# A decoder layer on one core: a second HBM accumulator for the routed experts, and their whole down product in rounded FP32

## The chip, the cores and the metric

The kernel runs on one core of a Trainium2 chip. The metric is the device time of one execution in microseconds (us), the median of 3 runs. One more execution was taken by the hardware profiler; the rows shown below come from it.

The engines are named as the profile names them: PE (TensorE, matrix products; PEld is its loading of weights), DVE (VectorE), ACT (ScalarE), POOL (GpSimd), SP (SyncE, which only issues DMAs here). A name with a q at its end, as ACTq, is the engine's sequencer.

## The reference, cut to what matters

One layer: attention, RWKV-7 and a gated MLP side by side, one output projection, and then a mixture of experts over 1024 tokens of width 1024. The change is in the mixture of experts, which computes this:

```python
scores = jax.nn.sigmoid(xt @ w_router)            # 64 experts
...                                               # top 8 of 64 per token, weights top_w
def expert_block(args):
    tok, e = args
    xb = xt[tok]
    hb = jax.nn.silu(xb @ w1[e]) * (xb @ w3[e])   # 1024 -> 256
    return hb @ w2[e]                             # 256 -> 1024
routed = zeros.at[row_tok].add(yb * row_w[:, None])
shared = (jax.nn.silu(xt @ ws1) * (xt @ ws3)) @ ws2
y = routed + shared
x = x + g2 * rmsnorm(y, norm_post_ffn)
```

All is FP32. The 8192 rows (1024 tokens, 8 experts each) are sorted by expert.

## The kernel before, in words

The stages follow one another: input projection, attention (`attend`), RWKV, then output projection, router and shared expert (`norm_route_experts`), and in the same program block the routed experts (`experts`), where the change is. A table `tab` in SBUF holds, for each block of 128 rows, its expert and the slot of its weights, and for each expert the number of blocks up to its end. Every engine runs its own loop of turns of four blocks, over as many turns as the table asks for: 24 turns or 96 blocks with these inputs, of which 95 have rows. 8 further turns are skipped by a branch. An engine reads the table with `value_load` (line 2327), which appears in the profile as TENSOR_LOAD on the engine's sequencer, with a few register instructions beside it.

Products are made exact enough in three passes: an operand is rounded to `fp32r` (its high part, by an ACT copy), DVE subtracts to get the low part, and PE adds high times high, high times low and low times high. The work of one block b is spread over several blocks' time:

- POOL gathers the block's 128 rows of `h2` from HBM (line 2377), four blocks ahead.
- PE transposes them (L2538), ACT copies the high part `xT_high` out of PSUM in two halves (L2404, L2405), DVE makes `xT_low` (L2484, L2485).
- The up weights `w13` (w1 and w3, 4096 columns) are rounded by ACT in four pieces of 1024 (L2411) and DVE makes four low pieces (L2470), two to three blocks ahead and into two sets of buffers.
- PE makes the up product, 24 products of 512 columns (L2546), the three passes interleaved for each of 8 contraction steps. It waits for all operands first.
- ACT applies Silu (L2423), DVE multiplies (L2491), PE transposes the result in two pieces (L2559). I take this L2559 as the start of a block on PE.
- Down product: contraction step 0 is one plain FP32 product per half of the output (L2568), with a DVE copy of the transposed activation (L2503) as operand. Step 1 is split (ACT L2415 and L2419, DVE L2476 and L2479) and takes three rounded passes per half (L2572).
- ACT copies the result out of PSUM (L2446, L2447), and POOL adds it to `acc` in HBM by an indirect DMA with addition (L2393). Each addition is issued only after the one before it has landed.

The weights of an expert (3 MB) lie in one of 4 slots. SP loads them in order of experts: it waits until the slot's old up weights have been split (`w_low`), issues four loads (L2585), waits until the down product of the slot's old expert is through (`dn_mm`, L2592's wait), issues two loads for w2, and waits for the up weights to land (L2345) before the next expert.

The order in a block's turn, by hand, is: PE transposes act(b), up(b+1), transposes x(b+2), down(b). ACT: operands of down(b), half of the split of w13(b+2), Silu(b+1), copy of x(b+2), half of the split of w13(b+3), copy of y(b). DVE: copies and indices for b, low parts of w13(b+2), the down operands in the middle of these, act(b+1), x(b+2).

At the end SP waits until 95 additions have landed and reads `acc` (L2363). DVE multiplies each of 8 tiles by the post-norm gain (L2519) and adds it to the residual (L2528), ACT makes the row norms (L2453 to L2455), and SP writes the tiles out (L2366).

## Time and profile before

| | |
|---|---|
| median of 3 runs | 1926.11 us |
| lowest and highest run | 1922.32 and 1934.88 us |
| span of the profiled execution, first to last instruction | 1924.1 us |
| PE busy, and PEld | 1746.1 us (91%), 1353.5 us (70%) |
| DVE busy | 1410.6 us (73%) |
| ACT busy | 1137.8 us (59%) |
| POOL busy | 465.8 us (24%) |
| HBM read, written | 333.82 MB, 82.13 MB |

The profile does not give a time for its own execution beside the span of 1924.1 us; that span lies inside the range of the three runs. A timeline row reads: start in us from the span's start, length in us, engine, line, operation, what is written and what is read, how many instructions the row merges, and in square brackets the idle time before it with what ended it. "issue" is a wait for nothing that the profile shows, so for the sequencer. Products on PE overlap, so it is the distance between starts that tells what one costs.

### The profile page before, as it was taken

The numbers are of one execution on the slowest core, as the hardware profiler recorded it, in microseconds if no ns is written. First come the engines' busy times: TensorE is split into PE (matmuls) and PEld (weight loads), VectorE is DVE, ScalarE is ACT, GpSimd is POOL, SyncE is SP. The second block draws the span as 40 slices with busy tenths as digits, with TensorE's granted clock in tenths as the row PEclk, the third lists the DMA queues.
The fourth block names the chain that finished last, engine by engine and source line by source line (L and its number), as shares of the span: only waits on it lengthen the run. The fifth ranks groups of instructions, "written<-read, shape, count | busy, mean of one in ns | idle before, by whom it ended". The sixth has DMA issues, their size and how long they took to land. (4 is left out here: it accounts for less than half of the span.)

```text
span 1924.1 us, 38146 instructions
## 1 busy us (share of the span) xinstructions
PE 1746.1 (91%) x10357; PEld 1353.5 (70%) x10358; DVE 1410.6 (73%) x2642; ACT 1137.8 (59%) x2188; POOL 465.8 (24%) x361
## 2 busy tenths in 40 slices
PE   3998999777599978998699999999999999999994
PEld 2787887555378756776577777777777677777773
DVE  6587651588478756666488888888888788888887
ACT  4411221477466543343477777777777677777776
POOL 0011100000022201336233333332333223333231
PEclk8999999999699978999799999999999999999997
DMA  9267610300200162428789978899888999899975
GB/s 358 82 197 208 199 53 28 130 16 17 93 6 8 33 232 77 111 79 173 243 266 294 298 220 277 252 311 332 266 260 292 315 302 284 259 285 300 316 233 194
DMA packets 132525, 380.04 MB, mean 198 GB/s; under 512 B 27365, under 2 KB 39998, under 8 KB 130380
## 3 DMA queue, kind: packets, MB, share of 16 engines
q1 hardware_dynamic: 97276, 288.36, 43.0%
q0 software_dynamic: 35168, 90.60, 19.5%
q8 instruction: 50, 0.82, 0.2%
q14 instruction: 31, 0.25, 0.0%
HBM read 333.82 MB, written 82.13 MB: 216 GB/s over the span
## 5 line engine op out<-in xcount | busy, mean ns | idle before, releaser
L2470 DVE TENSOR_TENSOR w_low<-w_experts,w_high 128x1024 fp32r<-128x1024 f32 x388 | 457.1, 1219 | 91.6 <-issue 63.4
L2411 ACT CAST w_high<-w_experts 128x1024 fp32r x390 | 390.0, 1049 | 94.8 <-issue 80.4
L2393 POOL DMA_INDIRECT acc<-y_rows,scatter_idx x96 | 185.0, 1927 | 604.8 <-DMA acc<-y_rows,scatter_idx 363.6
L2546 PE MATMUL rbank<-w_high,xT_high 128*128 128x512 f32 x776 | 314.7, 406 | 8.5 <-DVE xT_low L2485 8.5
L2546 PE MATMUL rbank<-w_high,xT_low 128*128 128x512 f32 x776 | 308.4, 397 | 0.0
L2546 PE MATMUL rbank<-w_low,xT_high 128*128 128x512 f32 x776 | 305.6, 394 | 0.0
L2568 PE MATMUL rbank<-w_experts,upper 128*128 x384 | 180.8, 593 | 1.9 <-DVE actT_low L2476 1.9
L2546 PEld LDWEIGHTS rbank<-w_high,xT_high 128*128 128x128 f32 x776 | 147.6, 190 | 40.2 <-DVE xT_low L2485 8.1
L2546 PEld LDWEIGHTS rbank<-w_high,xT_low 128*128 128x128 f32 x776 | 146.8, 189 | 33.4
L2546 PEld LDWEIGHTS rbank<-w_low,xT_high 128*128 128x128 f32 x776 | 147.4, 190 | 31.0
L2377 POOL DMA_INDIRECT gathered<-h,idx x96 | 137.5, 1432 | 44.5 <-issue 27.1
L2419 ACT CAST w_high<-w_experts 128x512 fp32r x192 | 110.3, 626 | 25.2 <-issue 22.5
L2479 DVE TENSOR_TENSOR w_low<-w_experts,w_high 128x512 fp32r<-128x512 f32 x192 | 123.2, 682 | 0.2
L2572 PE MATMUL rbank<-w_high,actT_high 128*128 128x512 f32 x192 | 113.9, 593 | 0.0
L2538 PEld LDWEIGHTS rbank<-ident,gathered 128*128 128x128 f32 x784 | 103.3, 192 | 11.1 <-DMA gathered<-h,idx 2.9
L1722 POOL DMA_INDIRECT lists<-ids,list_dest x64 | 70.0, 1094 | 165.3 <-DVE list_dest L1982 148.2
L525 PE MATMUL pbank<-w_in_high,hT_high 128*128 128x512 f32 x256 | 104.7, 409 | 2.2 <-DVE w_in_low L354 1.9
L2538 PE MATMUL rbank<-ident,gathered 128*128 128x128 f32 x784 | 104.0, 276 | 2.6 <-DMA gathered<-h,idx 2.6
L525 PE MATMUL pbank<-w_in_low,hT_high 128*128 128x512 f32 x256 | 102.3, 399 | 0.0
L525 PE MATMUL pbank<-w_in_high,hT_low 128*128 128x512 f32 x256 | 102.0, 398 | 0.0
L2568 PEld LDWEIGHTS rbank<-w_experts,upper 128*128 128x128 f32 x384 | 65.7, 191 | 48.0 <-issue 48.0
L932 POOL TENSOR_TENSOR r_k<-p_mixed,k 128x256 f32<-128x256 f32 x8 | 6.0, 747 | 341.3 <-DVE operands L1190 341.3
(445 smaller groups left out, 3611.7 us busy)
## 6 DMA issues: line engine op xcount, KB each, us to landing
w_experts<-in_exp_w SPq DMA_DIRECT2D x384, 512.0 KB
qT<-in_w_ada POOLq DMA_DIRECT2D x16, 1024.0 KB, 6.0
w_raw<-in_w_in SPq DMA_DIRECT2D x24, 512.0 KB, 6.8
w_ada<-in_w_ada SPq DMA_DIRECT2D x16, 512.0 KB, 15.1
p_mixed<-mixed SPq DMA_DIRECT2D x8, 512.0 KB, 8.4
w_out<-in_w_out SPq DMA_DIRECT2D x1, 4096.0 KB, 12.5
x_kept<-x SPq DMA_DIRECT2D x8, 512.0 KB
acc_tile<-acc SPq DMA_DIRECT2D x8, 512.0 KB, 7.1
```

The lines of the kernel that those rows point to most:

```text
L525: q = mm(bank[u % RING][:], lhs, rhs, start=(k == 0 and i == 0), stop=(k == KC - 1 and i == 2))
L1722: pool.indirect_dma_start(flat, bass.IndirectOffsetOnAxis(ap=w.dest[:, n:n + 1], axis=0), ids[:, t:t + 1], None).then_inc(lists_out[t % 2] ...
L2377: pool.indirect_dma_start(xg[j][:], None, dr["h2"], bass.IndirectOffsetOnAxis(ap=idx[j][:], axis=0), bounds_check=S - 1, oob_is_err=False) ...
L2393: pool.indirect_dma_start(dr["acc"], bass.IndirectOffsetOnAxis(ap=sidx[j][:], axis=0), y[j % 2][:], None, bounds_check=S - 1, oob_is_err=F ...
L2411: act.copy(w13_s[par][0][:, which, k], w13[:, bass.ds(w, 1), which, k].squeeze(1)).then_inc(w_high, 1)
L2419: act.copy(w2_s[half][0], w2[:, bass.ds(w, 1), 1, half * BANK:(half + 1) * BANK].squeeze(1)).then_inc(d_high, 1)
L2470: dve.tensor_tensor(w13_s[par][1][:, which, k], w13[:, bass.ds(w, 1), which, k].squeeze(1), w13_s[par][0][:, which, k], ALU.subtract).then ...
L2479: dve.tensor_tensor(w2_s[half][1], w2[:, bass.ds(w, 1), 1, half * BANK:(half + 1) * BANK].squeeze(1), w2_s[half][0], ALU.subtract).then_in ...
L2538: q = pe.transpose(ps_x[k // 4][:, (k % 4) * P:(k % 4 + 1) * P], xg[j][:, 0:D].rearrange("p (c k) -> p k c", k=KC)[:, k, :], ident[:])
L2546: q = pe.matmul(ps_h[:].rearrange("p (a n) -> p a n", a=2), xT[a][:, k, :], w13_s[par][z][:, :, k, :], start=(k == 0 and m == 0), stop=(k ...
L2568: pe.matmul(ps_y[n][:], aT[:], w2[:, bass.ds(w, 1), 0, n * BANK:(n + 1) * BANK].squeeze(1), start=True, stop=False)
L2572: q = pe.matmul(ps_y[n][:], aT_s[a][:], w2_s[n][z], start=False, stop=(m == 2))
```

## The change

Five things change, all in or for `experts`:

1. A second accumulator `acc1` in HBM takes the rows of odd blocks. Each addition now waits for the one two blocks before it, which went to the same accumulator. `acc1` is set to zero during attention, by 8 DMAs of 512 KB on SP's queue from a tile that DVE clears. At the end SP reads both accumulators (16 tiles), and DVE adds them before it multiplies.
2. The whole down product is rounded: w2 is split in full (2048 columns, was 1024), both steps of the transposed activation too, and PE makes 12 rounded products for a block in place of 2 plain and 6 rounded ones. The DVE copies L2503 and L2506 (scatter indices) go; the index tile now holds a scatter and a gather column, filled by one copy.
3. Operations are merged: w13 in two pieces of 2048 columns, x and y in one copy of 1024, w2 in one of 2048, on ACT and on DVE. The copy of the slot weights (L2486) moves from DVE to ACT.
4. PE takes the passes with low parts last, in the up product (high·high for all 8 steps, then high·low, then low·high) and in the down product, and waits for each operand only ahead of its pass.
5. ACT copies y(b-1) after the operands of down(b), in the next block's turn. SP waits for DVE's low part of w2 (`d_low`) before it overwrites w2, and no more for the product. The `tab` is flat, PE reads it no more, buffers move, and the SBUF space for descriptors of POOL's DMAs is set to 8192 bytes.

```diff
+            sp.wait_ge(zero_done, 1)
+            for t in range(NT):
+                sp.dma_start(dr["acc1"][t * P:(t + 1) * P, :], zero[:]).then_inc(zero_out, 16)
...
+            dve.memset(zero[:], 0.0).then_inc(zero_done, 1)
...
-                sp.wait_ge(dn_mm, sp.value_load(tab[0:1, 2, bass.ds(after, 1)], min_val=1, max_val=BLOCKS) + 1)
+                sp.wait_ge(d_low, sp.value_load(tab[0:1, bass.ds(after + ENDS, 1)], min_val=1, max_val=BLOCKS))
...
-        sp.wait_ge(y_out, n_blocks(sp) * 16)
+        nb = n_blocks(sp)
+        sp.wait_ge(y_out[1], nb // 2 * 16)
         for t in range(NT):
-            sp.dma_start(acc_tile[t][:], dr["acc"][t * P:(t + 1) * P, :]).then_inc(acc_in[t], 16)
+            sp.dma_start(acc_tile[t][:], dr["acc1"][t * P:(t + 1) * P, :]).then_inc(acc_in[t], 16)
+        sp.wait_ge(y_out[0], (nb + 1) // 2 * 16)
...
+        sp.wait_ge(dn_mm, (nb + 3) // 4 * 4 + 1)
+        for t in range(NT):
+            sp.dma_start(acc1_tile[t][:], dr["acc"][t * P:(t + 1) * P, :]).then_inc(acc1_in[t], 16)
...
-                    pool.wait_ge(y_ready, b + 2)
-                    pool.sem_inc(held, 1)
-                    pool.wait_ge(y_out, b * 16)
+                    pool.wait_ge(y_out[j % 2], (i * 2 + j // 2) * 16)
                     pool.sem_inc(y_free, 1)
-                    pool.indirect_dma_start(dr["acc"], bass.IndirectOffsetOnAxis(ap=sidx[j][:], axis=0), y[j % 2][:], None,
-                                            bounds_check=S - 1, oob_is_err=False, compute_op=ALU.add).then_inc(y_out, 16)
+                    pool.wait_ge(y_ready, b + 2)
+                    pool.sem_inc(held, 1)
+                    pool.indirect_dma_start(sums_of[j % 2], bass.IndirectOffsetOnAxis(ap=idx[j][:, 0:1], axis=0), y[j % 2][:], None,
+                                            bounds_check=S - 1, oob_is_err=False, compute_op=ALU.add).then_inc(y_out[j % 2], 16)
...
+            act.copy(xT[0][:], k8(ps_x)).then_inc(x_copied, 1)
+            act.copy(wslot[j][:], xg[j][:, bass.ds(expert_of(act, n) + D, 1)]).then_inc(xw_ready, 1)
...
+            e, w = expert_of(act, n), slot_of(act, n)
+            act.wait_ge(w13_ready, e + 1)
+            for a in which:
+                act.copy(w13_s[par][0][:, a], w13[:, bass.ds(w, 1), a].squeeze(1)).then_inc(w_high, 2)
...
+            act.wait_ge(dn_mm, n + 1)
+            act.copy(w2_s[0][:], w2[:, bass.ds(w, 1)].squeeze(1)).then_inc(d_high, 1)
...
+                    split_rest(b + 2, j % 2, range(1))
+                    act_rest(b)
+                    indices(i, j)
                     down_rest(b)
-                    split_rest(b + 2, j % 2, (2, 3))
+                    split_rest(b + 2, j % 2, range(1, 2))
                     activate(b + 1, (j + 1) % 4)
-                    x_rest(b + 2, (j + 2) % 4)
+                    x_rest(b + 2)
...
             dve.wait_ge(acc_in[t], 16)
+            dve.wait_ge(acc1_in[t], 16)
+            dve.tensor_tensor(acc_tile[t][:], acc_tile[t][:], acc1_tile[t][:], ALU.add).then_inc(f_added, 1)
+            dve.wait_ge(f_added, t + 1)
             dve.tensor_tensor(acc_post[t][:], acc_tile[t][:], post[:], ALU.mult).then_inc(posted, 1)
...
+            pe.wait_ge(x_copied, n + 1)
+            pe.wait_ge(w_high, n * 4 + 4)
+            up_pass(n, par, 0, 0)
             pe.wait_ge(w_low, n * 4 + 4)
+            up_pass(n, par, 0, 1)
             pe.wait_ge(x_low, n + 1)
+            up_pass(n, par, 1, 0).then_inc(up_mm, 1)
```

The order of the instructions in the loop, at two places. First ACT, from its copy of x(b+2) to its split of w13(b+3). Before, this is the copy in two halves, two reads of the table, and the first pieces of the split:

```order
L2404 CAST xT_high<-rbank 128x512
L2405 CAST xT_high<-rbank 128x512
L2327 ISA
L2327 TENSOR_LOAD tab
L2327 ISA x3
L2327 TENSOR_LOAD tab
L2327 ISA x2
L2409 REGISTER_ALU
L2411 ISA
L2411 COPY w_high_7992<-w_experts 128x1024
L2411 ISA
L2411 COPY w_high_7992<-w_experts 128x1024
```

Now one copy stands there, with a read of the table and the copy of the slot weights behind it, and then two more reads; the split in one piece of 2048 columns comes right after these rows:

```order
L2429 CAST xT_high<-rbank 128x1024
L2339 TENSOR_LOAD tab
L2339 ISA x2
L2430 ISA
L2430 COPY slot_w_8009<-gathered_4447 128x1
L2339 ISA
L2339 TENSOR_LOAD tab
L2339 ISA x2
L2342 ISA
L2342 TENSOR_LOAD tab
L2342 ISA x2
L2434 REGISTER_ALU
```

So the number of table reads between the copy of x and the split goes from two to three, and the copy `slot_w` is new on ACT.

Second PE, in the down product. Before: two plain products of 512 columns (the operand `upper` holds the transposed activation), then three rounded ones for each half.

```order
L2568 ISA
L2568 MATMUL rbank<-w_experts,upper 128x512
L2568 ISA
L2568 MATMUL rbank<-w_experts,upper 128x512
L2570 ISA
L2572 MATMUL rbank<-w_high_7985,actT_high 128x512
L2572 MATMUL rbank<-w_low,actT_high 128x512
L2572 MATMUL rbank<-w_high_7985,actT_low 128x512
L2570 REGISTER_ALU
L2572 MATMUL rbank<-w_high_7986,actT_high 128x512
L2572 MATMUL rbank<-w_low,actT_high 128x512
L2572 MATMUL rbank<-w_high_7986,actT_low 128x512
```

Now, from the transposes of the activation through the up product to the down product:

```order
L2604 MATMUL rbank<-ident,act 128x128 x2
L2564 REGISTER_ALU
L2565 ISA
L2574 MATMUL rbank<-w_high_8004,xT_high 128x512 x8
L2574 MATMUL rbank<-w_low_8005,xT_high 128x512 x8
L2574 MATMUL rbank<-w_high_8004,xT_low 128x512 x8
L2558 ISA
L2560 MATMUL rbank<-ident,gathered_4449 128x128 x8
L2590 MATMUL rbank<-w_high,actT_high 128x512 x4
L2590 MATMUL rbank<-w_high,actT_low 128x512 x4
L2590 MATMUL rbank<-w_low,actT_high 128x512 x4
```

All 12 products of the down product are rounded, the low part of w2 is needed last, and the table reads ahead of the down product are gone from PE.

## Rows read from the trace of the kernel before

**Rows 1.** Stretches of the span: us, busy us per engine (instructions), clock, DMA share, GB/s.
```profile
1000.00:1100.00 100.00, 100.00 (x453) 77.01 (x453) 84.14 (x143) 77.63 (x123) 33.23 (x20) 1.00 0.95 295
...
1500.00:1600.00 100.00, 95.38 (x424) 72.28 (x424) 81.11 (x136) 75.59 (x121) 27.59 (x19) 1.00 0.93 313
```

**Rows 2.** Timeline of PE's weight loads: L2559, the first of each block; start us, us.
```profile
941.41 0.31 PEld L2559 LDWEIGHTS rbank<-ident,act 128*128 128x128 f32 x2 [1.62 <-DVE act L2491]
...
1408.58 0.20 PEld L2559 LDWEIGHTS rbank<-ident,act 128*128 128x128 f32 x1
...
1428.12 0.20 PEld L2559 LDWEIGHTS rbank<-ident,act 128*128 128x128 f32 x1
...
1885.87 0.20 PEld L2559 LDWEIGHTS rbank<-ident,act 128*128 128x128 f32 x1
```

**Rows 3.** Timeline of PE in one down product: plain FP32 loads, then rounded products.
```profile
1406.13 0.19 PEld L2568 LDWEIGHTS rbank<-w_experts,upper 128*128 128x128 f32 x1 [0.24 <-issue]
1406.56 0.19 PEld L2568 LDWEIGHTS rbank<-w_experts,upper 128*128 128x128 f32 x1 [0.24 <-issue]
...
1417.71 0.39 PE L2572 MATMUL rbank<-w_high,actT_low 128*128 128x512 f32 x1
1417.94 0.39 PE L2572 MATMUL rbank<-w_high,actT_high 128*128 128x512 f32 x1
```

**Rows 4.** Timeline of ACT over one block.
```profile
1415.72 0.59 ACT L2404 CAST xT_high<-rbank 128x512 fp32r<-128x512 f32 x1 [0.45 <-PE rbank L2538]
...
1417.20 2.00 ACT L2411 CAST w_high<-w_experts 128x1024 fp32r x2 [0.41 <-issue]
...
1419.11 0.58 ACT L2446 COPY y_rows<-rbank 128x512 f32<-128x512 f32 x1
...
1420.06 0.28 ACT L2415 CAST actT_high<-rbank 128x128 fp32r<-128x128 f32 x1
1420.87 1.14 ACT L2419 CAST w_high<-w_experts 128x512 fp32r x2 [0.53 <-issue]
```

**Rows 5.** Timeline of DVE over one block.
```profile
1410.65 2.36 DVE L2470 TENSOR_TENSOR w_low<-w_experts,w_high 128x1024 fp32r<-128x1024 f32 x2 [0.78 <-ACT w_high L2411]
...
1413.13 1.28 DVE L2479 TENSOR_TENSOR w_low<-w_experts,w_high 128x512 fp32r<-128x512 f32 x2
...
1416.61 0.47 DVE L2491 SCALAR_TENSOR_TENSOR act<-act,slot_w,rbank 128x256 f32<-128x256 f32 x1
```

**Rows 6.** Line 2327, 950 to 1890 us: operation, count, ns min/median/max, first and last start.
```profile
L2327 ACTq TENSOR_LOAD <-tab x570: 272/280/1525, 952.8 to 1888.5; - x190
```

**Rows 7.** Timelines of POOL, and of ACT behind its copy of x.
```profile
1406.10 1.40 POOL L2377 DMA_INDIRECT gathered<-h,idx  x1 [0.30 <-issue]
...
1408.13 2.00 ACT L2411 CAST w_high<-w_experts 128x1024 fp32r x2 [1.15 <-issue]
...
1513.19 1.99 ACT L2411 CAST w_high<-w_experts 128x1024 fp32r x2 [6.69 <-SPq L2345]
```

**Rows 8.** Waits in the loop: groups of POOL, then the SP queue (us, times, longest).
```profile
L2393 POOL DMA_INDIRECT acc<-y_rows,scatter_idx x96 | 185.0, 1927 | 604.8 <-DMA acc<-y_rows,scatter_idx 363.6 <-issue 151.0 <-PE rbank L2538 44.1
...
SPq L2345 <- DMA w_experts<-in_exp_w: 245.7, 40, 11.3
SPq L2592 <- PE rbank L2572: 210.1, 29, 16.3
```

**Rows 9.** Timelines of the end: POOL, SP's queue, DVE.
```profile
1889.49 2.28 POOL L2393 DMA_INDIRECT acc<-y_rows,scatter_idx  x1 [5.46 <-issue]
1892.08 1.66 POOL L2377 DMA_INDIRECT gathered<-h,idx  x1 [0.30 <-issue]
...
1896.35 3.76 SPq L2363 DMA_DIRECT2D acc_tile<-acc  x8
...
1901.69 2.36 DVE L2519 TENSOR_TENSOR acc_post<-acc_tile,post 128x1024 f32<-128x1024 f32 x2 [6.07 <-issue]
...
1918.51 2.47 DVE L2528 SCALAR_TENSOR_TENSOR x_kept<-acc_post,f_stats,x_kept 128x1024 f32<-128x1024 f32 x2
```

More of the change, by code:

```diff
@@ L649, in _ @@
             sp.wait_ge(mixed_in, 16 * NT)
+            sp.wait_ge(zero_out, 16 * NT)
         @block.scalar
@@ L2282, in experts @@
     xg01, xg23 = XG_AT[0], XG_AT[2]
-    w2_low = at("w2_low", [P, 2, BANK], xg01 + 2 * row, F32R)
-    w2_high = [at(f"w2_high{n}", [P, BANK], xg01 + 2 * row + (2 + n) * BANK * 4, F32R) for n in range(2)]
+    w2_s = [keep["w2_high"], at("w2_low", [P, FC, D], xg01 + 2 * row, F32R)]
     sg = at("act", [P, F], xg01 + 2 * row + 4 * BANK * 4)
@@ L2293, in experts @@
     assert half1 + 5 * D * 4 <= xg23
-    aT_s = [at("actT_high", [P, P], W_OUT_AT + 8 * D * 4, F32R), at("actT_low", [P, P], small, F32R)]
-    wslot = [at(f"slot_w{j}", [P, 1], small + P * 4 + j * 32) for j in range(4)]
-    sidx = [at(f"scatter_idx{j}", [P, 1], small + P * 4 + (4 + j) * 32, I32) for j in range(4)]
-    assert small + P * 4 + 8 * 32 <= W_OUT_AT and W_OUT_AT + 8 * D * 4 + P * 4 <= 224 * 1024
-    aT = keep["upper"]
-    w2_s = [[w2_high[n][:], w2_low[:, n]] for n in range(2)]
@@ L2301, in experts @@
-    PASSES = ((0, 0), (0, 1), (1, 0))
-    PIECES = [(which, slice(half * KC // 2, (half + 1) * KC // 2)) for which in range(2) for half in range(2)]
-    bank = keep["rbank"]
-    ps_x, ps_y, ps_h, ps_a = bank[0:2], bank[2:4], bank[4], bank[5:5 + FC]
+    aT_s = [at("actT_high", [P, FC, P], w13_at + 8 * D * 4, F32R), keep["actT_low"]]
+    wslot = [at(f"slot_w{j}", [P, 1], small + j * 32) for j in range(4)]
+    assert small + 4 * 32 <= w13_at and w13_at + 8 * D * 4 + FC * P * 4 < 224 * 1024
+    banks = keep["rbank"]
@@ L2315, in experts @@
+    y_out, sums_of = [sem(f"e_y_out{j}") for j in range(2)], [dr["acc"], dr["acc1"]]
     TURNS = (BLOCKS + 3) // 4
+    slots_at = keep["parts_at"]
     post, x2 = keep["post2"], [keep["x2"][t // 4][:, t % 4, :] for t in range(NT)]
@@ L2423, in silu, with y_copy @@
             act.activation(sg[:], ps_h[:, 0:F], ACT.Silu).then_inc(silu_done, 1)
-        x_copy(0)
+        def y_copy(n, j):
+            act.wait_ge(y_free, n + 3)
+            act.wait_ge(dn_mm, n + 2)
+            act.copy(y[j % 2][:].rearrange("p (b n) -> p b n", b=2), ps_y).then_inc(y_ready, 1)
+        x_copy(0, 0)
         act.wait_ge(x2_out[1], 8 * NT)
-        split(1, 1, PIECES)
+        split(1, 1, range(2))
         act.wait_ge(acc_out[0], 8 * NT)
         silu(0)
-        x_copy(1)
-        split(2, 0, PIECES[:2])
+        x_copy(1, 1)
+        split(2, 0, range(1))
         act.wait_ge(acc_out[1], 8 * NT)
@@ L2457, in vector @@
     def vector(dve):
-        step = Steps(dve, dve_step)
         dve.wait_ge(tab_done, 1)
         nb = n_blocks(dve)
-        def index(n, j):
-            dve.tensor_copy(idx[j][:], lists[:, bass.ds(n, 1)]).then_inc(idx_ready, 1)
-        def split_rest(n, par, pieces):
-            w = entry(dve, 1, n, SLOTS - 1)
-            for m in pieces:
-                which, k = PIECES[m]
-                dve.wait_ge(w_high, n * 4 + m + 1)
-                dve.tensor_tensor(w13_s[par][1][:, which, k], w13[:, bass.ds(w, 1), which, k].squeeze(1),
-                                  w13_s[par][0][:, which, k], ALU.subtract).then_inc(w_low, 1)
@@ L2482, in x_rest, with indices, split_rest @@
-        def x_rest(n, j):
+        def indices(i, j):
+            dve.wait_ge(y_free, i * 4 + j + 1)
+            dve.tensor_copy(idx[j][:], list_turns[:, j, bass.ds(i, 2)]).then_inc(idx_ready, 1)
+        def split_rest(n, par, which):
+            w = slot_of(dve, n)
+            for a in which:
+                dve.wait_ge(w_high, n * 4 + 2 * a + 2)
+                dve.tensor_tensor(w13_s[par][1][:, a], w13[:, bass.ds(w, 1), a].squeeze(1), w13_s[par][0][:, a],
+                                  ALU.subtract).then_inc(w_low, 2)
@@ L2639, in build @@
         sb = lambda n, s: ctx.enter_context(nc.sbuf_tensor(n, s, F32))
-        keep = {"spent": [], "ident": sb("ident", [P, P]), "upper": sb("upper", [P, P]), "eps": sb("eps", [P, 4])}
+        w2_high = ctx.enter_context(nc.sbuf_tensor("w2_high", [P, FC, D], F32R))
+        keep = {"spent": [], "w2_high": w2_high, "ident": sb("ident", [P, P])}
+        keep["upper_at"] = nc.sbuf_base
+        keep["upper"] = sb("upper", [P, P])
+        keep["eps"] = sb("eps", [P, 4])
         with ExitStack() as qkv:
@@ L2660, in build @@
         keep["idx_ready"] = ctx.enter_context(nc.semaphore("idx_ready"))
-        keep["idx"] = [ctx.enter_context(nc.sbuf_tensor(f"idx{j}", [P, 1], mybir.dt.int32)) for j in range(4)]
+        keep["idx"] = [ctx.enter_context(nc.sbuf_tensor(f"idx{j}", [P, 2], mybir.dt.int32)) for j in range(4)]
         keep["xg_in"], keep["acc_out"] = ([ctx.enter_context(nc.semaphore(f"{n}{j}")) for j in range(m)] for n, m in (("xg_in", 4), ("acc_out", 2)))
```

186 lines of the change are left out of this document (98 added, 88 removed).

## The prediction

> **What bounds the kernel now.** I read the busy time by stretches first, since the change lies in one stage. In a full stretch of the routed experts PE is busy 100.00 of 100 us at full granted clock, DVE 84, ACT 78; the DMA engines stand at 0.95 [rows 1]. So PE bounds, and the transfers are close behind. Four of the nine stretches of 100 us from 1000 us on stand at 0.93 or more; in the one at 1500 us PE loses 4.6 us.
>
> Then the starts of the blocks on PE. Two undisturbed blocks take 1428.12 - 1408.58 = 19.54 us, so 9.77 each. From the first block's start to that of the 96th it is 1885.87 - 941.41 = 944.5 us [rows 2]; 95 times 9.77 is 928.2, so 16 us are stalls.
>
> Then the timelines of ACT and DVE over one block. There the reader is to see how much room is left before PE: DVE writes the activation for the next block at 1416.61 and needs 0.47 us [rows 5], PE takes it at 1418.4, so 1.3 us of room. Last the waits: POOL waits 364 us for additions to land [rows 8], but nobody on the path waits for POOL much. The sequencers' table reads (TENSOR_LOAD) take 280 ns at the median but up to 1525 [rows 6].
>
> **The PE work.** A plain product of 512 columns costs two steps of 0.43 us, a rounded one 0.23 [rows 3]. Out go 2 plain products, 4 x 0.43 = 1.72 us; in come 6 rounded ones more, 6 x 0.23 = 1.38. That leaves PE 9.77 - 0.34 = 9.43 us a block. The passes in another order are the same 24 products.
>
> **Whether DVE and ACT can follow.** Both get more work: 1024 more columns of w2 each. ACT: two pieces of 1024 take 2.00 us, two of 512 take 1.14 [rows 4]; so 0.84 ns a column and 0.1 fixed, and a piece of 2048 takes 1.90 with a distance of 1.82 to the next. DVE: 2.36 and 1.28 for the pairs [rows 5], 1.05 ns a column, so 2.22 from one piece of 2048 to the next. Merging saves little, since back-to-back pieces overlap already.
>
> I count from a block's start on PE, as 1408.58 in rows 2. ACT starts its copy of x(b+2) 1415.72 - 1408.58 = 7.14 later; that follows from PE's transposes and stays. From there to the split of w13 it is 1.48 us with two table reads [rows 4], of which each has about 0.65 with its register instructions; with the third read the split starts at 9.25 and ends at 11.15. DVE's low part of it: 11.2 to 13.4. The low activation (256 columns, 128 take ACT 0.28 [rows 4]; 0.35) and the indices: 13.85. Low w2: 16.05. ACT meanwhile: activation 11.5, w2 to 13.4, y at 0.9 (halves 0.5 each in rows 4) to 14.3, other half of w13 to 16.2. DVE's low part of that: 16.3 to 18.5, activation to 18.95, PE starts block b+2 at 19.0. That is a chain over two blocks, 9.5 a block, as long as PE's own 9.43. The 1.3 us of room are gone; what is late next is this chain. I take 9.5: 95 x 0.27 = **-26 us**. Bounds: 9.43 gives -32, and 9.65 (0.15 more in the chain, the error of my slopes and reads) -11.
>
> DVE itself is occupied 2.22 x 3 + 0.35 + 0.1 + 0.4 + 1.15 = 8.7 us a block and ACT, with its wait for reads, 9.3; so neither bounds by work alone, but ACT nearly.
>
> **Table reads held up.** Some reads take over a microsecond. At 1406.10 POOL issues a gather; ACT's split after it starts with 1.15 us of idle time, 0.74 more than the 0.41 a block later [rows 7, 4]. Before, this fell into ACT's and DVE's room. Now an extra microsecond on ACT goes to PE undiminished. When does it happen? POOL issues the gather 2.6 us after the addition [rows 9]; with y copied at 4.8 after the block's start, the addition goes at 5.7 and the gather at 8.3, when the third read (8.4) begins. Before it was 6.2 against reads at 7.2 and 7.8. So the read falls on the edge of the gather. I take one block in eight, 12 x 0.7 = **+8 us**; bounds 0 and 38 (two blocks in five, 1 us each).
>
> The Trainium skill (DMA: Bandwidth & Descriptors, Latency and other measured facts) puts a floor of about 600 ns under a `tensor_load`. The median of 280 ns over 570 reads [rows 6] stands against it here, and the measurement decides; by the page three reads would cost 0.96 us more than I count.
>
> **Weights.** At 1513.19 ACT had waited 6.69 us for up weights [rows 7]. SP waits 245.7 us for them to land, and 210.1 in 29 waits for the down product before it may load w2 [rows 8]. The second wait now ends some 3 us earlier (DVE's low w2 is done at 16.05 - 9.5 = 6.5 of the block, the product ended at its end). The other way, a block that comes sooner asks for its weights sooner, and the slot's up weights are let go at 9.0 of a block, where it was 8.1 (1416.7); and the room that swallowed 1.3 us of each such wait is gone. Bounds -10 and +20; I take **+4**.
>
> **Second accumulator.** It removes POOL's wait of 364 us, but that hid under PE but for a few blocks; its gain is within the 16 us of stalls. With it go PE's two table reads a block, and the wait of the first blocks for the low part of x: together **-4**, bounds 0 and -12.
>
> **The end.** The output y(94) is copied at 4.8 of block 95 and its addition issued at 5.7; landing takes 1896.35 - 1889.49 = 6.9 us [rows 9], so the second set of loads goes at 12.6 after the last block's start. It was 1896.35 - 1885.87 = 10.5 [rows 2, 9]. The first set is loaded earlier, under the last block. DVE started at 15.8 then, held by its sequencer ("issue", 6.07), and the tile arrives about 4 us after its issue now, at 16.6: +0.8. Then DVE is the bound: its 8 tiles took 1920.98 - 1901.69 = 19.3 us [rows 9], and an addition of the same 1024 columns is 1.22, with the wait for its own result 1.28: 8 x 1.28 = 10.2. Together **+11**; bounds +8 and +15 (the loads late by as much as the whole 4 MB).
>
> **At nothing:** the clearing of `acc1` in attention (8 DMAs that take SP 3.8 us to issue, as in rows 9; the first output of attention has two buffers; bound +4), the clearing of its tile on DVE (no more than the 1.2 us of an operation of as many columns), the merged index copy, and the smaller descriptor space of POOL's DMAs, for which no row has a price (POOL idles 604.8 us [rows 8]; bound +10 in the 64 list scatters).
>
> **Sum:** -26 + 8 + 4 - 4 + 11 = -7 us. It is made against the profiled execution, whose span of 1924.1 us stands 2 under the median of 1926.1; so 1926 - 7 = **1919 us**. 1% is 19 us, about what a measurement of this kernel can tell from no change.
>
> **Rivals.**
> *The pipeline runs clean.* No long read meets the chain, and three quarters of the 16 us of stalls go, since additions and w2 loads wait less: -26 - 12 + 11 = -27, so 1899. For it: the gather comes after most reads. Against it: weights make the largest stall.
> *The weights set the pace.* The dense stretches keep their length, so only 5/9 of the 26 us come, 14; stalls grow by 8, long reads cost 4 beside them: -14 - 4 + 8 + 4 + 11 = +5, so 1931. For it: 0.93 to 0.95 [rows 1]. Against it: SP's 210 us of waits are cut.
> *ACT's chain is hit (slower).* If the read falls into the gather in two blocks of five at 1 us, 38 us are lost: -26 - 4 + 38 + 4 + 11 = +23, so 1949. The change turns slower once held reads cost over 15 us, 0.16 a block. For it: reads of 1.1 us and more occur, and ACT has 0.1 to 0.2 us to spare. Against it: the gather has to come a few tenths earlier than I reckon.
> *All reads are long (slower too).* If each read on ACT takes 0.32 us more than its median, its cycle of 9.3 becomes 10.3: 95 x 0.5 + 11 = +59, 1985. This is what the page's floor would make of it; the median of rows 6 is against it.
>
> **Chances.** Forecast 0.35, clean 0.30, weights 0.20, ACT hit 0.13, all reads long 0.02. Faster by over 1% (under 1907) is most of the clean case and the low edge of the forecast: 0.31. Slower by over 1% (over 1945): the last two and the upper edge of the weights' case, 0.15. Between: 0.54. The range leaves out the tail of either side: 1895 to 1943.
>
> **What would show it.** Right: starts of undisturbed blocks 9.4 to 9.6 us apart; rounded products only, 12 in 2.8 us; DVE's activation just ahead of PE's transposes, with PE waiting there; no waits for additions; the end about 11 us longer from the last block's start. Wrong: blocks at 9.7 or more with ACT idle behind its copy of x ("issue"); more than 16 us of stalls with waits on SP's up weights; a longer attention stage.

## The result and the profile after

| kernel | median us | runs | ratio to before, 95% interval |
|---|---|---|---|
| before | 1926.11 | 1922.32 to 1934.88 | 1 |
| changed | 1935.35 | 1929.4 to 1937.55 | 1.0046 [1.0026, 1.0066] |
| changed, measured again beside the experiments | 1929.39 | 1921.42 to 1936.21 | 1.0013 [0.9990, 1.0037] |

The forecast was 1919 us, 7 us less than before; measured was 2 to 9 us more, each time against the kernel before in the same session. That is inside 1% and inside the range, but on the other side of no change. The first interval excludes no change and the second includes it, so how much slower the changed kernel is stays uncertain between nothing and 0.7%; that it is not 7 us faster (a ratio of 0.9964) both intervals show.

I split both profiled executions (spans 1924.1 and 1933.5 us) at the first and the last block's start on PE.

| part | before | changed | difference | forecast |
|---|---|---|---|---|
| ahead of the first block | 941.4 | 957.2 | +15.8 | 0 |
| first to last block start (95 intervals) | 944.5 | 923.6 | -20.9 | -26 + 8 + 4 - 4 = -18 |
| last block start to the end of the span | 38.2 | 52.7 | +14.5 | +11 |

So the loop as a whole came out near the forecast. The end cost 3.5 us more, and 16 us were lost where I had written nothing; 9.9 of them are traced to their cause below.

**The loop.** PEld's rows of the changed kernel give the block starts, as [rows 2] for before: the first and the 96th. The bracket is the idle time ahead of each.

```profile
957.22 0.32 PEld L2604 LDWEIGHTS rbank<-ident,act 128*128 128x128 f32 x2 [1.63 <-DVE act L2516]
...
1880.78 0.31 PEld L2604 LDWEIGHTS rbank<-ident,act 128*128 128x128 f32 x2 [0.50 <-DVE act L2516]
```

The timeline of all engines over the two blocks that start at 1393.09 and 1402.71 holds the chain of the prediction. It answers to [rows 4, 5].

```profile
1393.09 0.32 PEld L2604 LDWEIGHTS rbank<-ident,act 128*128 128x128 f32 x2 [0.28 <-DVE act L2516]
...
1400.12 1.02 ACT L2429 CAST xT_high<-rbank 128x1024 fp32r<-128x1024 f32 x1
...
1402.18 1.90 ACT L2436 CAST w_high<-w_experts 128x2048 fp32r x1 [0.95 <-issue]
...
1406.85 2.28 DVE L2507 TENSOR_TENSOR w_low<-w_experts,w_high 128x2048 fp32r<-128x2048 f32 x1
1407.30 1.91 ACT L2436 CAST w_high<-w_experts 128x2048 fp32r x1
...
1409.37 2.29 DVE L2497 TENSOR_TENSOR w_low<-w_experts,w_high 128x2048 fp32r<-128x2048 f32 x1 [0.24 <-ACT w_high L2436]
...
1411.58 0.47 DVE L2516 SCALAR_TENSOR_TENSOR act<-act,slot_w,rbank 128x256 f32<-128x256 f32 x1
1411.97 1.22 DVE L2511 TENSOR_TENSOR xT_low<-rbank,xT_high 128x1024 fp32r<-128x1024 f32 x1
1412.11 0.32 PEld L2604 LDWEIGHTS rbank<-ident,act 128*128 128x128 f32 x2
```

Counted from 1393.09: x copy at 7.0 (forecast 7.14), split at 9.1 (9.25), low w2 done at 16.0 (16.05), other half on ACT done at 16.1 (16.2), its low part at 18.6 (18.5), activation at 19.0 (18.95), PE at 19.02 (19.0). These two blocks are 9.5 us each; the mean of all is 923.6 / 95 = 9.72.

The view of waits, from 950 to 1880 us, shows that PE waits for almost nothing but the activation, and that POOL waits for no addition any more (363.6 us in [rows 8]). A stall of PE can appear at PEld and at PE both, so the two rows are not added:

```profile
POOL acc L2418 <- ACT y_rows L2453: 485.9, 89, 7.9
...
ACT w_high L2436 <- issue: 77.8, 84, 1.6
ACT w_high L2444 <- issue: 48.9, 80, 1.5
PEld rbank L2604 <- DVE act L2516: 37.2, 78, 1.8
...
PE rbank L2604 <- DVE act L2516: 10.2, 20, 1.4
```

**Ahead of the loop.** Attention's outputs `o` on DVE, before (L736) and changed (L743); the last row of each pair is the third output. Kernel before:

```profile
371.77 0.34 DVE L736 SCALAR_TENSOR_TENSOR o<-ps_o,soft_stats,subln 128x128 f32<-128x128 f32 x1
375.57 0.35 DVE L736 SCALAR_TENSOR_TENSOR o<-ps_o,soft_stats,subln 128x128 f32<-128x128 f32 x1 [1.02 <-ACT soft_stats L679]
```

Changed kernel, DVE and then SP's queue:

```profile
371.49 0.34 DVE L743 SCALAR_TENSOR_TENSOR o<-ps_o,soft_stats,subln 128x128 f32<-128x128 f32 x1
384.83 0.35 DVE L743 SCALAR_TENSOR_TENSOR o<-ps_o,soft_stats,subln 128x128 f32<-128x128 f32 x1 [10.56 <-DMA ymix<-o]
```

```profile
360.18 4.47 SPq L645 DMA_DIRECT2D p_mixed<-mixed  x8
364.70 6.29 SPq L648 DMA_DIRECT2D acc<-zero_rows  x8
371.03 18.98 SPq L651 DMA_DIRECT2D ymix<-o  x4
```

The first output is issued at 371.03 (367.97 before, since SP takes 6.3 us to issue the clearing), behind 4 MB of zeros, and landed 13.7 us later, at 384.7; the median of all 32 outputs is 1.6 us. The third output needs its buffer. Both kernels stand at the same time until 371.5; the third output is then 9.3 us late and the load of `w_out` (497.6 and 507.4) 9.8. That is most of the 15.8.

The transfers show what the first output stood behind. The 4 MB of `mixed` that SP loads from 360.18 on were not through either when the zeros came. The stretch from 375 to 380 us, the kernel before in the first line and the changed one in the second (the last two columns are the busy share of the DMA engines and GB/s):

```profile
375.00:380.00 5.00, 3.29 (x21) 1.64 (x17) 4.17 (x8) 3.50 (x14) 0.00 (x0) 1.00 0.05 13
...
375.00:380.00 5.00, 0.21 (x4) 0.02 (x2) 0.00 (x0) 1.35 (x6) 0.00 (x0) 0.86 1.03 420
```

From 365 to 380 us the changed kernel moves 419 to 420 GB/s with the DMA engines always busy. Added up, some 9.4 MB moved from 360 to 384.7 us, 8.4 of them these loads and zeros; at 384.7 the first output landed. Whether the output had to wait for its place in SP's queue or only for a share of busy DMA engines, no run tells apart: none issues the zeros from another queue.

The rest of the 15.8, 6.0 us, lies between the load of `w_out` and the first block (443.8 and 449.8 us). In the other twelve profiles the same stretch took 443.8 to 447.1 us, and 446.3 when the changed kernel ran again, so how much of these 6.0 us belongs to the change stays open.

**The end.** The timeline of the changed kernel's end, SP, POOL and DVE; L2418 at 1886.71 adds the output of the last of the 95 blocks. It answers to [rows 9].

```profile
1883.81 3.89 SPq L2379 DMA_DIRECT2D acc_tile<-acc  x8
1886.71 2.13 POOL L2418 DMA_INDIRECT acc<-y_rows,idx  x1 [5.47 <-ACT y_rows L2453]
...
1897.56 3.82 SPq L2388 DMA_DIRECT2D acc_tile<-acc  x8
1901.52 1.22 DVE L2539 TENSOR_TENSOR acc_tile<-acc_tile,acc_tile 128x1024 f32<-128x1024 f32 x1 [9.90 <-DMA acc_tile<-acc]
...
1907.51 1.22 DVE L2539 TENSOR_TENSOR acc_tile<-acc_tile,acc_tile 128x1024 f32<-128x1024 f32 x1
...
1911.10 1.22 DVE L2539 TENSOR_TENSOR acc_tile<-acc_tile,acc_tile 128x1024 f32<-128x1024 f32 x1
```

The kernel before, the same distance between two tiles on DVE:

```profile
1905.72 1.22 DVE L2519 TENSOR_TENSOR acc_post<-acc_tile,post 128x1024 f32<-128x1024 f32 x1
...
1908.05 1.22 DVE L2519 TENSOR_TENSOR acc_post<-acc_tile,post 128x1024 f32<-128x1024 f32 x1
```

DVE takes 1911.10 - 1907.51 = 3.59 us a tile, where it took 2.33. It starts 1901.52 - 1880.78 = 20.7 us after the last block's start; before, 15.8. From the issue of the addition at 1886.71 to SP's next load it is 1897.56 - 1886.71 = 10.9 us, with the first set's 4 MB loading beside it; before, it was 6.9 [rows 9]. (The expectations below say 10.3 for it, counted to the end of SP's wait.) From here on landing is counted to SP's next load.

### The profile page after: what moved, and what is told of

It is laid out like the page before. It is cut to its first block, busy times and chain, and to the rows that moved or that the text cites. A ratio compares the mean times of both kernels' runs of the same rounds, so it can differ in the third digit from the quotient of the medians.

```text
span 1933.5 us, 35045 instructions
## 1 busy us (share of the span) xinstructions
PE 1726.5 (89%) x10549; PEld 1381.7 (71%) x10549; DVE 1473.2 (76%) x1973; ACT 1185.0 (61%) x1802; POOL 522.2 (27%) x361
## 3 DMA queue, kind: packets, MB, share of 16 engines
q0 software_dynamic: 35168, 90.60, 18.6%
## 4 chain that ended last, share of the span: by engine, by line
PE 28%; ACT 9%; DMA 8%; issue 7%; ACTq 7%; DVE 2%; SPq 1%; DVEq 1%; POOL 1%; POOLq 0%
PE rbank L2574 13%; DMA w_experts<-in_exp_w 5%; PE rbank L2135 5%; ACT w_high L2436 5%; PE rbank L2590 4%; ACTq L2342 3%; ACTq L2339 3%; PE rbank L2560 2%; ACT y_rows L2453 2%; DMA lists<-ids,list_dest 2%; PE rbank L2174 1%; PE rbank L2604 1%; POOL lists L1731 1%; PE rbank L2221 1%; SPq L2620 1%
## 5 line engine op out<-in xcount | busy, mean ns | idle before, releaser
L2497 DVE TENSOR_TENSOR w_low<-w_experts,w_high 128x2048 fp32r<-128x2048 f32 x194 | 444.5, 2292 | 80.0 <-ACT w_high L2436 79.1
L2436 ACT CAST w_high<-w_experts 128x2048 fp32r x195 | 372.1, 1909 | 95.4 <-issue 79.5
L2418 POOL DMA_INDIRECT acc<-y_rows,idx x96 | 211.4, 2202 | 527.1 <-ACT y_rows L2453 497.5
L2507 DVE TENSOR_TENSOR w_low<-w_experts,w_high 128x2048 fp32r<-128x2048 f32 x96 | 219.7, 2289 | 14.3 <-ACT w_high L2444 13.3
L2444 ACT CAST w_high<-w_experts 128x2048 fp32r x96 | 183.5, 1912 | 51.1 <-issue 49.7
L2574 PE MATMUL rbank<-w_high,xT_high 128*128 128x512 f32 x776 | 205.5, 407 | 1.1 <-issue 1.1
L2574 PE MATMUL rbank<-w_low,xT_high 128*128 128x512 f32 x776 | 195.6, 394 | 0.0
L2574 PE MATMUL rbank<-w_high,xT_low 128*128 128x512 f32 x776 | 194.6, 393 | 0.0
L2511 DVE TENSOR_TENSOR xT_low<-rbank,xT_high 128x1024 fp32r<-128x1024 f32 x98 | 119.2, 1216 | 7.8 <-ACT xT_high L2429 7.8
L2429 ACT CAST xT_high<-rbank 128x1024 fp32r<-128x1024 f32 x98 | 99.8, 1018 | 13.2 <-PE rbank L2560 10.8
L2590 PE MATMUL rbank<-w_high,actT_low 128*128 128x512 f32 x384 | 104.9, 395 | 0.0
L2590 PE MATMUL rbank<-w_low,actT_high 128*128 128x512 f32 x384 | 104.8, 394 | 0.0
## 6 DMA issues: line engine op xcount, KB each, us to landing
acc<-zero_rows SPq DMA_DIRECT2D x8, 512.0 KB, 13.7
```

The lines of the kernel that those rows point to most:

```text
L2418: pool.indirect_dma_start(sums_of[j % 2], bass.IndirectOffsetOnAxis(ap=idx[j][:, 0:1], axis=0), y[j % 2][:], None, bounds_check=S - 1, oob ...
L2429: act.copy(xT[0][:], k8(ps_x)).then_inc(x_copied, 1)
L2436: act.copy(w13_s[par][0][:, a], w13[:, bass.ds(w, 1), a].squeeze(1)).then_inc(w_high, 2)
L2444: act.copy(w2_s[0][:], w2[:, bass.ds(w, 1)].squeeze(1)).then_inc(d_high, 1)
L2497: dve.tensor_tensor(w13_s[par][1][:, a], w13[:, bass.ds(w, 1), a].squeeze(1), w13_s[par][0][:, a], ALU.subtract).then_inc(w_low, 2)
L2507: dve.tensor_tensor(w2_s[1][:], w2[:, bass.ds(w, 1)].squeeze(1), w2_s[0][:], ALU.subtract).then_inc(d_low, 1)
```

## The experiments

Twelve runs followed, one of them of the changed kernel as it is. The profile of each was split as above; "attention" is the time from SP's load of `p_mixed` to that of `w_out`. The stage ahead of attention has the same code everywhere and took 353 to 361 us from one execution to another, so I compare parts. The runs fell into three sessions, in which the median of the kernel before was 1925.2, 1927.1 and 1926.1 us; times of different sessions are therefore compared by their ratios.

| run | median us | ratio to before | attention | loop | end |
|---|---|---|---|---|---|
| before, its profile | 1926.1 | 1 | 137.3 | 944.5 | 38.2 |
| changed, its profile | 1935.4 | 1.0046 | 147.2 | 923.6 | 52.7 |
| e8_after_again | 1929.4 | 1.0013 [0.9990, 1.0037] | 151.1 | 922.5 | 53.3 |
| e2_clear_spread | 1916.1 | 0.9954 [0.9933, 0.9974] | 137.9 | 920.6 | 52.4 |
| e3_before_ring | 1925.1 | 1.0001 [0.9979, 1.0023] | 137.5 | 939.6 | 38.8 |
| e1_one_acc | 1942.6 | 1.0086 [1.0058, 1.0114] | 137.6 | 968.9 | 38.5 |
| e7_before_two | 1932.1 | 1.0018 [1.0002, 1.0033] | 137.5 | 937.1 | 49.6 |
| e9_up_order | 1964.1 | 1.0205 [1.0179, 1.0231] | 148.7 | 957.7 | 53.1 |
| e10_down_order | 1930.4 | 1.0040 [1.0022, 1.0058] | 148.8 | 923.1 | 53.4 |
| e4_act_first | 1911.4 | 0.9932 [0.9910, 0.9954] | 149.0 | 904.3 | 54.5 |
| e5_spread_first | 1901.2 | 0.9857 [0.9838, 0.9875] | 138.5 | 905.9 | 53.9 |
| e6_end_late | 1899.4 | 0.9849 [0.9828, 0.9870] | 139.0 | 905.8 | 51.5 |
| e11_pe_sum | 1898.2 | 0.9868 [0.9845, 0.9892] | 137.4 | 908.4 | 51.2 |
| e12_pe_sum_half | 1898.9 | 0.9868 [0.9847, 0.9889] | 137.9 | 905.7 | 52.3 |

**The clearing elsewhere (e2_clear_spread).**

```diff
-            for t in range(NT):
-                sp.dma_start(dr["acc1"][t * P:(t + 1) * P, :], zero[:]).then_inc(zero_out, 16)
             for i, (h, n) in enumerate(ITEMS):
                 sp.wait_ge(o_ready, i + 1)
                 sp.dma_start(dr["ymix"]...
+                if i % 3 == 2 and i // 3 < NT:
+                    sp.dma_start(dr["acc1"][i // 3 * P:(i // 3 + 1) * P, :], zero[:]).then_inc(zero_out, 16)
```

> The changed kernel; the eight stores that clear the second accumulator are issued one behind every third output of attention instead of all ahead of the first. Theory A (the third output of attention waited 10.6 us on VectorE for the landing of the first, which lay behind 4 MB of clearing): that wait goes, the first list scatter is back from 768.5 to about 758.9, and the time falls by 9 to 10 us to about 1926 us. Theory C (something else in attention got longer, the place of the stores does not matter): no change, 1935 us. Each output then still lies behind one 512 KB store: under 1 us each if at all.

Theory A. Attention is back to 137.9 us, POOL's first list scatter (after RWKV and the router) to 758.4 us. The third output of this kernel, on DVE, is where it was before:

```profile
375.43 0.35 DVE L745 SCALAR_TENSOR_TENSOR o<-ps_o,soft_stats,subln 128x128 f32<-128x128 f32 x1 [1.02 <-ACT soft_stats L687]
```

Nine profiles without the clearing up front show 137.3 to 139.0 us for attention, five with it 147.2 to 151.1. This kernel writes the same 4 MB as the changed one. By the ratios the time fell by 0.6% (11 us) against the changed kernel measured again (1.0013) and by 0.9% (18 us) against its first measurement (1.0046), where 9 to 10 were expected; attention alone gives 13.2 and 9.3 us against their profiles.

**One accumulator again (e1_one_acc).** No clearing, no second set, and each addition waits for the one before it:

```diff
                     pool.wait_ge(y_ready, b + 2)
-                    pool.indirect_dma_start(sums_of[j % 2], ...
+                    pool.wait_ge(y_out[(j + 1) % 2], (i * 2 + (j + 1) // 2) * 16)
+                    pool.indirect_dma_start(dr["acc"], ...
```

> The changed kernel with one accumulator again: no clearing in attention, every addition goes to the first accumulator behind the landing of the one before it, no second set of tiles and no additions at the end. Theory A (the second accumulator costs 9.6 us in attention and 14.5 us at the end, and gives the loop nothing): start of the first block back from 957.2 to about 947.5, last block start to end of the span back from 52.7 to 38-40 us, loop still about 924 us, in all 1935.4 - 24 = 1911 us. Theory B (the loop's gain of 20.9 us comes from additions that need not wait for each other): the loop grows back to 935-945 us and the time is 1921-1931 us. Theory C (the memory layout, not the clearing, moved the start): first block stays at 955-957, time about 1921 us.

Theory A fell, and hard: attention and end came back as it said, but the loop grew by 45 us and took all of it. Theory B had the direction and at most half of the size. Its waits from 950 to 1880 us:

```profile
POOL acc L2408 <- DMA acc<-y_rows,idx: 433.6, 69, 10.0
...
PEld rbank L2591 <- DVE act L2506: 54.4, 65, 2.6
...
ACT y_rows L2443 <- POOLq L2403: 42.8, 27, 3.5
...
PE rbank L2591 <- DVE act L2506: 32.2, 29, 2.2
...
PEld rbank L2547 <- DMA gathered<-h,idx: 22.4, 22, 2.5
```

And POOL's timeline, where transfers are dense:

```profile
1547.75 3.59 POOL L2408 DMA_INDIRECT acc<-y_rows,idx  x1 [7.67 <-DVE idx L2481]
...
1560.07 2.42 POOL L2408 DMA_INDIRECT acc<-y_rows,idx  x1 [7.39 <-DMA acc<-y_rows,idx]
1562.79 1.03 POOL L2390 DMA_INDIRECT gathered<-h,idx  x1 [0.30 <-issue]
1571.30 3.65 POOL L2408 DMA_INDIRECT acc<-y_rows,idx  x1 [7.47 <-DVE idx L2481]
```

Additions follow each other every 11 to 12.5 us there. (`DVE idx`, named in two rows, is nothing that an addition waits for in the program: it waits for its copied output and for landings.) In 69 waits over the loop POOL waited for the landing of the last addition, 433.6 us in all. A late addition holds two things up. POOL's program has the gather and the release of the output buffer behind it, so ACT, which copies the output in the midst of its splits, waits 42.8 us for the buffer (in the changed kernel the list has no such wait); what it does later comes later, and the waits for the activation grow from 37.2 to 54.4 us at PEld and from 10.2 to 32.2 at PE. And rows are gathered late: PEld waits 22.4 us for them.

**The second accumulator at the old pace (e7_before_two).** The kernel before, with the additions alternating, the clearing spread and the sum at the end; blocks keep 9.77 us.

> The kernel before with the second accumulator alone (cleared in pieces behind the outputs of attention, summed at the end): blocks keep their 9.77 us. Theory P (at the old pace the landing of additions hardly binds; it does only once a block is shorter): the loop gains 4 to 10 of 944 us, the end is 14 us longer, time 1930-1936 us. Theory Q (the second accumulator brings the loop some 20 us or more at any pace, by freeing the queues): loop 920-925 us, time 1918-1922 us.

Theory P. The loop is 937.1 us, 7 less than in the profile of before and 2.5 less than in that of e3; POOL's waits for landing (420.8 us in e3) are gone and bring almost nothing, the end costs 11. So the same part is worth 2 to 7 us of loop in the kernel before, at 9.77 us a block, and 45 in the changed one, at 9.5. The pace is not all that differs: in e1 ACT copies the output a block's turn later, and POOL releases the buffer at another place of its program. No run parts the pace from this order.

**The smaller descriptor space (e3_before_ring).** The kernel before with `dynamic_dma_scratch_size=8192` and 8 KB of SBUF left empty.

> The kernel before with only the smaller descriptor space for GpSimd's transfers (8192 instead of 16384, the room left empty). Theory R (the smaller space is what makes the list scatters land later and the scatter and gather take longer on GpSimd): first block starts at 944-948 instead of 941.4, GpSimd's additions take about 2.2 us instead of 1.93 and gathers 1.75 instead of 1.43, time 1929-1932 us. Theory S (it costs nothing; the 6 us ahead of the loop and the longer GpSimd operations come from what they run beside): 941 to 942, 1.93 and 1.43 us, time 1926 us within 2.

Theory S: 1.0001. The addition took 1.91 us on POOL and the gather 1.39, no more than before (1.93 and 1.42). From the load of `w_out` to the first block it took 446.7 us here, 443.8 before and 449.8 in the changed kernel, but 446.3 when that was run again: what moves these few microseconds stays open.

**The pass orders (e9_up_order, e10_down_order).** The changed kernel, with PE waiting for all low parts ahead of the first pass of the up or of the down product:

```diff
-            up_pass(n, par, 0, 0)
             pe.wait_ge(w_low, n * 4 + 4)
-            up_pass(n, par, 0, 1)
             pe.wait_ge(x_low, n + 1)
-            up_pass(n, par, 1, 0).then_inc(up_mm, 1)
+            for k in range(KC):
+                for a, z in ((0, 0), (0, 1), (1, 0)):
+                    q = pe.matmul(...)
```

> The changed kernel with the three products of the up projection interleaved again for each piece of 128 rows, so that TensorE needs both low parts at once. Theory O (the pass order is part of the gain: VectorE's low part of x now ends some 1.1 us after the block's start, TensorE asks for it 0.3 after it): TensorE waits 0.8 us more per two-block chain of 19.0 us, block 9.9 us, loop 955-965 us instead of 923, time 1965-1975 us. Theory Z (as the prediction had it, the order is worth nothing in the steady blocks): loop 920-926 us, time 1929-1936 us.

Theory O, 34 us of loop. The waits of e9, from 960 to 1900 us, name it, L2511 being the low part of x:

```profile
PE rbank L2569 <- DVE xT_low L2511: 31.8, 67, 0.7
ACT xT_high L2429 <- PE rbank L2560: 30.0, 73, 0.5
```

> The changed kernel; the down projection waits for the low activation and the low w2 before its first pass instead of before its second and third. VectorE ends the low w2 16.05 us after a block's start by the prediction's count, 6.6 after the next one's; TensorE comes to the down product 6.8 after its block's start. Theory O2 (order needed): the low part is late by up to 0.8 us in most blocks, loop 930-1000 us. Theory Z2 (just in time): loop 920-930 us, time 1930-1940 us.

Theory Z2: 923.1 us of loop. The low w2 ends 16.0 after a block's start, 6.5 after the next one's, and PE comes for it at 6.7: just in time. In e10 PE waits for it in ten blocks, 6.7 us in all, but the loop is as long as without this wait (923.1 and 923.6).

**The activation first (e4_act_first).** On DVE:

```diff
                     down_rest(b)
+                    activate(b + 1, (j + 1) % 4)
                     split_rest(b + 2, j % 2, range(1, 2))
-                    activate(b + 1, (j + 1) % 4)
                     x_rest(b + 2)
```

> The changed kernel; VectorE computes the activation of the next block ahead of the low part of the second half of the up weights, no longer behind it. Theory K (the chain over ScalarE's second half, its low part and the activation holds TensorE: 48 us of TensorE's waits in the loop are for the activation): those waits all but go, undisturbed blocks start 9.3 to 9.45 us apart, the loop shrinks from 923.6 by 10 to 25 us, time 1912-1925 us. Theory L (ScalarE, with its reads of the table, or the transfers set the pace anyway): the waits of TensorE move to the low up weights or to gathered rows, the loop stays within 5 us of 923.6, time 1931-1936 us.

Theory K. The waits for the activation fall from 37.2 us to 1.6 at PEld and from 10.2 to 1.4 at PE; in e4, from 950 to 1880 us:

```profile
ACT w_high L2436 <- issue: 70.9, 83, 1.2
...
PEld rbank L2604 <- DVE act L2516: 1.6, 1, 1.6
...
PE rbank L2604 <- DVE act L2516: 1.4, 1, 1.4
```

ACT still loses time ahead of its split, where its table reads stand ("issue" at L2436, 70.9 us against 77.8 in the changed kernel), but it no longer reaches PE: the activation is written at 1401.86, PE takes it at 1403.99.

```profile
1401.86 0.48 DVE L2516 SCALAR_TENSOR_TENSOR act<-act,slot_w,rbank 128x256 f32<-128x256 f32 x1 [0.57 <-ACT act L2448]
...
1403.99 0.44 PEld L2604 LDWEIGHTS rbank<-ident,act 128*128 128x128 f32 x2
```

Blocks are 9.52 and 9.42 us in turn, 9.47 on the mean: this is PE's own length. 904.3 us are 95 x 9.47 and 4.6 us of stalls. The pass order allows this: the low weights are now done at 1404.99, and PE starts the up product at 1404.38 but takes its first low pass only at 1406.11 (two numbers of the same timeline). Whether the old order would spoil it was not run.

**Both (e5_spread_first).**

> Both edits at once: the clearing spread behind the outputs of attention, and the activation ahead of the second low half. If the two gains lie in different stages and add up: first block near 944, loop near 904, end 52-55 us, time 1900-1904 us, 1.2% under the kernel before. If one hid the other (both acting on the same stall): no better than the 1911 of the second edit alone.

They add up: attention 138.5 us, loop 905.9, a ratio of 0.9857, which the two effects taken from the changed kernel's two measurements put at 0.984 to 0.987.

**The end (e6_end_late, e11_pe_sum, e12_pe_sum_half).** All on top of e5. e6 loads nothing until the last additions have landed, then both sets pair by pair; e11 lets PE add six tiles, as products with the identity:

```diff
+        for t in range(4):
+            pe.wait_ge(acc_in[t], 16)
+            sum_part(t, acc_tile, True)
+        for t in PE_TILES:
+            ...
+            pe.wait_ge(acc1_in[t], 16)
+            sum_part(t, acc1_tile, False).then_inc(f_pe, 1)
```

> As the run before it, but both sets of tiles are loaded at the end, pair by pair, only when the last additions have landed. Theory M (the 4 MB of the first set, read while the last addition is under way, made its landing 10.3 us instead of 6.9): the addition lands 3 us sooner, VectorE's first addition starts no later than the 20.7 us after the last block's start, the end is 50-53 us long, the time is that of the run before it within 3 us. Theory N (the early set is worth its time, the landing is late for another reason): the landing stays at 10 us, the tiles come 4-8 us later and the time is 4-8 us longer.

Theory M. In e6 the addition lands 1865.50 - 1858.35 = 7.1 us after its issue; in e5 it took 11.4 (1850.36 to 1861.72), and 10.7 to 11.7 in the nine profiles with the early 4 MB:

```profile
1858.35 2.22 POOL L2420 DMA_INDIRECT acc<-y_rows,idx  x1 [4.28 <-ACT y_rows L2455]
...
1865.50 0.32 SPq L2389 DMA_DIRECT2D acc_tile<-acc  x1
...
1870.45 1.22 DVE L2541 TENSOR_TENSOR acc_tile<-acc_tile,acc_tile 128x1024 f32<-128x1024 f32 x1 [6.59 <-DMA acc_tile<-acc]
```

DVE starts 19.0 us after the last block's start, where it was 21.9. The early loads bought nothing: the end is 2.4 us shorter without them. The times of e5 and e6 can't be told apart.

> Both edits of the fifth run; besides, at the end TensorE adds the two accumulators of six of the eight tiles in its banks (products with the identity), VectorE only those of tiles 5 and 7. Theory D (the end is bound by VectorE's three operations a tile, 3.59 us): six tiles at 2.4 us, the end 53.9 - 6 x 1.2 = 46-49 us, time 1893-1896 us. Theory T (the tiles' transfers bound it as soon as VectorE is quicker): the end stays at 52-54 us with VectorE waiting for the transfers, time 1899-1902 us.

> As the run before it, with only half of the first set loaded early, the other half pair by pair with the second set: the last addition shares its time with 2 MB instead of 4. By theory M (early loads delay the last addition by 3 to 4 us per 4 MB) it lands 1.5-2 us sooner than in the run before; by theory T the late pairs (1 MB a tile) hold VectorE in the second half and the gain is lost. 1892-1896 us if M decides, 1896-1900 us if T does.

In e11 neither theory came out as written. Tiles on PE do go through DVE in 2.33 us (1877.90 to 1880.23), but the path to the first of them is longer (PE's products, then ACT's squares, then DVE; the program lets ACT and DVE read a tile's banks in turn), and DVE starts at 25.9 instead of 21.9:

```profile
1870.43 1.02 ACT L2488 ACTIVATE acc_squares<-rbank 128x1024 f32<-128x1024 f32 x1 [7.74 <-PE rbank L2623]
...
1871.68 1.23 DVE L2546 TENSOR_TENSOR acc_post<-rbank,post 128x1024 f32<-128x1024 f32 x1 [13.48 <-ACT acc_squares L2488]
...
1877.90 1.22 DVE L2546 TENSOR_TENSOR acc_post<-rbank,post 128x1024 f32<-128x1024 f32 x1
...
1880.23 1.22 DVE L2546 TENSOR_TENSOR acc_post<-rbank,post 128x1024 f32<-128x1024 f32 x1
```

Six tiles save 6 x 1.26 = 7.6 us, 4.0 are given back at the start, and the end is 2.7 us shorter than in e5. In e12 only 2 MB are loaded early, and the landing lies between the two others, 1867.19 - 1858.14 = 9.1 us:

```profile
1858.14 2.22 POOL L2424 DMA_INDIRECT acc<-y_rows,idx  x1 [4.28 <-ACT y_rows L2459]
...
1867.19 2.90 SPq L2394 DMA_DIRECT2D acc_tile<-acc  x4
```

So with nothing, 2 MB and 4 MB beside it the same addition took 7.1, 9.1 and 10.7 to 11.7 us: theory M's mechanism holds. The time fell into theory T's band all the same, since DVE started at 27.1. e5, e6, e11 and e12 can't be told apart by their ratios; each runs 1.3 to 1.5% faster than the kernel before, and so faster than both kernels.

> The changed kernel again, beside the others on one chip. 1933-1937 us, 0.4-0.5% over the kernel before, as measured first; its front (to the first list scatter) may differ by 5 us either way from one execution to another, as the profiles of the same code have shown: 768.5 and 773.5.

It came out at 1929.4, under the band: the median of one session stands 6 us off that of another, and the ratio moves from 1.0046 to 1.0013. Its profile has the same parts as the first: attention 151.1, loop 922.5, end 53.3 us.

## Why the prediction was wrong, by its own steps

1. **At nothing: the clearing of `acc1` (bound +4).** This step failed. I priced SP's issue time, 3.8 us (it measured 6.3), and argued that the output has two buffers. I didn't ask when the first output *lands* with 4 MB of zeros, and 4 MB of loads, ahead of it: 13.7 us after its issue, while the outputs come some 4 us apart. Attention paid 147.2 - 137.3 = 9.9 us in the first profile, 11.4 to 13.8 in the four others. Without it (e2) the ratio is 0.9954, where the forecast was 0.9964; that they agree so closely is partly luck, since the errors of the end and of the loop cancel. "A longer attention stage" stood in the list of what would prove it wrong.
2. **The end, +11.** Half of it right: the additions on DVE cost 8 x 1.26 = 10.1 (forecast 10.2). Its start came 4.9 us late where I had +0.8. The mis-sized term is the landing of the last addition, taken as 6.9 us from before [rows 9]; with the first set loading beside it, it measured 10.9. e6 and e12 show the cause: 7.1 without the early loads, 9.1 with half of them.
3. **PE work and chain, -26.** Right: 9.5 us for each of the two blocks followed above; each step of the chain within 0.2 us; PE's own length 9.47 (forecast 9.43), seen in e4.
4. **Held-up reads +8 and weights +4.** With these the forecast left 16 - 4 + 8 + 4 = 24 us of stalls in the loop; measured were 923.6 - 95 x 9.5 = 21. With no room on DVE disturbances reach PE; with 1.7 us of room (e4) only 5 us do. The split between the two terms is not what I wrote. In the trace of the changed kernel three blocks (11.26, 10.52 and 12.15 us, from 1285.51, 1508.99 and 1519.51 on) follow waits of ACT for up weights of 3.30, 2.55 and 4.17 us: 5.4 us above 9.5. The other 15.6 us lie in some forty blocks of 9.65 to 10.36 us, a few tenths each, where I had one block in eight at 0.7. In most of them ACT idles by "issue" ahead of its splits; no run shows that the reads are the cause. So the total is near for a mechanism whose sizes I had wrong, which is luck in part.
5. **Second accumulator, -4.** About right for the kernel before (e7: 2 to 7 us), but not what the part is worth in the changed kernel: 45 us (e1). It didn't spoil the sum, since the chain of 9.5 us was reckoned without these waits. Had the question been which part to leave out, the answer would have been wrong.
6. **Pass order, "the same 24 products".** True for PE and silent on the waits: DVE ends the low x 1.1 us after the block's start, which the interleaved order can't stand. Worth 34 us (e9), only for the up product (e10). My chain to 19.0 rested on it unsaid.
7. **Descriptor space, at nothing.** Right (e3).

Of the rivals, none came true. "The weights set the pace" named 1931 us, nearest to what was measured, but by another way: it had the loop gain 6 us, and it gained 20.9. The sum of the forecast's errors: +16 ahead of the loop, of which 10 is the clearing and 6 is open, +3.5 at the end, -3 in the loop.

## What to carry to other kernels

Price an added transfer by when the next small one behind it lands, not by its issue time: megabytes put ahead of a double-buffered output stall the engine that fills it; spread them. A part that is worth little in one kernel may carry the next one (here 2 to 7 us and 45), so judge parts of a joint change together, one left out at a time. When PE's own time and a chain through two engines come out equal, look for an operation on the chain whose consumer can wait, and put the urgent one ahead of it; that gave 19 us here.
